# Reordering the engines' queues at two seams of a two-layer decoder trunk, and halving one operand's hand-over

## The reference, cut to what matters

```
h = rms_norm(x, norm_mix_pre);  proj = h @ w_in;   y = [gmlp | retention | swa](proj)
x = x + rms_norm(y @ w_out, norm_mix_post)
h = rms_norm(x, norm_ffn_pre)
x = x + rms_norm((silu(h @ w_gate) * (h @ w_up)) @ w_ffn_out, norm_ffn_post)
x = x + sigmoid(x @ w_ple_gate) * rms_norm(p @ w_ple_proj, ple_norm)
```

## Time and profile before

| | |
|---|---|
| median of 3 runs | 1254.16 us (1253.76 to 1254.63) |
| the profiled execution's own time | 1254.62 us |
| its span in the profile | 1252.1 us |
| busy in the span | PE 1238.4 (99%), PEld 1137.0 (91%), DVE 786.0 (63%), ACT 571.0 (46%), POOL 126.5 (10%) |
| granted TensorE clock | 0.999 of full speed, mean |

### The profile page before, as it was taken

The page is one execution under the profiler, slowest core; times in us unless marked ns, Lnnn a source line. Parts: engine busy times, 40 slices in busy tenths (PEclk is TensorE's granted clock), DMA queues, the critical chain, the costliest instruction groups (busy, mean ns, idle before and its releaser), DMA issues.

```text
span 1252.1 us, 20527 instructions
## 1 busy us (share of the span) xinstructions
PE 1238.4 (99%) x8045; PEld 1137.0 (91%) x8045; DVE 786.0 (63%) x1321; ACT 571.0 (46%) x1084; POOL 126.5 (10%) x225
## 2 busy tenths in 40 slices
PE   9999999999999999999999999999999999999998
PEld 8999887999999988887899989879999999888876
DVE  5675545888888843346466756367988887532463
ACT  6444334555555532235454444353655555322341
POOL 2003521000000000001120037020000000000010
PEclk9999999999999999999999999999999999999999
DMA  7322232233333353423231222222333333523111
GB/s 247 102 66 88 68 101 68 69 102 102 102 109 111 104 167 101 135 68 97 68 98 60 89 64 90 80 81 71 102 103 114 106 102 103 171 89 126 68 51 67
DMA packets 124206, 122.30 MB, mean 98 GB/s; under 512 B 5200, under 2 KB 109008, under 8 KB 124112
## 3 DMA queue, kind: packets, MB, share of 16 engines
q1 hardware_dynamic: 124112, 121.01, 31.4%
HBM read 118.90 MB, written 2.10 MB: 97 GB/s over the span
## 4 chain that ended last, share of the span: by engine, by line
PE 77%; DVE 3%; ACT 2%; issue 1%; POOL 1%; ACTq 0%; DVEq 0%; POOLq 0%
PE bank L799 25%; PE bank L800 24%; PE bank L801 24%; PE bank L989 1%; DVE upd L1838 1%; DVE x L1845 1%; DVE w_lo L1599 1%; PE bank L1046 0%; PE bank L1069 0%; ACT junk L1334 0%; PE bank L1115 0%; POOL tiny L1498 0%; ACT w_hi L1185 0%; ACT junk L1212 0%; PE bank L1067 0%
## 5 line engine op out<-in xcount | busy, mean ns | idle before, releaser
L799 PE MATMUL bank<-w_hi,h_hi 128*128 128x384 f32 (+2 forms) x672 | 244.2, 363 | 1.8 <-DVE ple_n L1838 1.0
L800 PE MATMUL bank<-w_lo,h_hi 128*128 128x384 f32 (+2 forms) x672 | 237.5, 353 | 0.0
L1599 DVE TENSOR_TENSOR w_lo<-raw,w_hi 128x1024 fp32r<-128x1024 f32 x86 | 102.5, 1231 | 157.1 <-ACT w_hi L1185 156.9
L801 PE MATMUL bank<-w_hi,h_lo 128*128 128x384 f32 (+2 forms) x576 | 200.4, 348 | 0.0
L1185 ACT ACTIVATE w_hi<-raw 128x1024 fp32r<-128x1024 f32 x86 | 86.7, 1053 | 181.2 <-PE bank L801 181.1
L799 PE MATMUL bank<-h_hi,w_hi 128*128 128x256 f32 x568 | 161.2, 284 | 3.0 <-issue 1.9
L801 PE MATMUL bank<-h_hi,w_lo 128*128 128x256 f32 x568 | 160.7, 283 | 0.0
L800 PE MATMUL bank<-h_lo,w_hi 128*128 128x256 f32 x568 | 160.7, 283 | 0.0
L799 PEld LDWEIGHTS bank<-w_hi,h_hi 128*128 128x128 f32 x672 | 126.4, 188 | 16.2 <-issue 1.8
L801 PE MATMUL bank<-w_hi,mid_lo 128*128 128x512 f32 x352 | 137.0, 389 | 0.0
L800 PEld LDWEIGHTS bank<-w_lo,h_hi 128*128 128x128 f32 x672 | 126.6, 188 | 10.6
(11 more groups left out here) (235 smaller groups left out, 2662.8 us busy)
## 6 DMA issues: line engine op xcount, KB each, us to landing
raw<-in_w_ffn_in SPq DMA_DIRECT2D x88, 512.0 KB, 3.9
raw<-in_w_ffn_out SPq DMA_DIRECT2D x44, 512.0 KB, 3.4
raw<-in_w_in SPq DMA_DIRECT2D x40, 384.0 KB, 3.8
raw<-in_w_out SPq DMA_DIRECT2D x16, 512.0 KB, 4.0
raw<-in_w_gate SPq DMA_DIRECT2D x16, 512.0 KB, 4.2
raw<-in_w_in SPq DMA_DIRECT2D x10, 512.0 KB, 4.0
raw<-in_w_ple SPq DMA_DIRECT2D x4, 512.0 KB, 4.8
x<-in_x_in SPq DMA_DIRECT2D x3, 512.0 KB, 7.1
```

What stands on the lines that cost most here:

```text
L799: pe.matmul(out_ap, a_hi, b_hi, start=start, stop=False, skip_group_check=True)
L800: pe.matmul(out_ap, a_hi, b_lo, start=False, stop=False, skip_group_check=True)
L801: return pe.matmul(out_ap, a_lo, b_hi, start=False, stop=stop, skip_group_check=True)
L1599: last = dve.tensor_tensor(lo, raw[q % RAWS][:, cols], hi, ALU.subtract)
```

## The change

It moves events in the list, and changes waits:

1. First seam: `conv ffn1` comes before `pre ffn 2` (it was behind it); `post mix 3` comes before `hraw 1`.
2. DVE's `h_lo` of `T ffn 1` is taken out of its own place and put inside `post mix 2`, between the two scaling instructions and the addition to x.
3. The normed tile `xn` is written in two instructions of 512 columns, each with its signal, and PE's transposes wait half by half.
4. `mm_ffn` waits for each of the strip's two pieces and for each half of the tokens' channels (k 0 to 3, k 4 to 7) as it comes to them.
5. Second seam: `conv gate1` moves from behind `T gate 2` to behind `post ple 1`; `conv gate2` from in front of `post ple 2` to behind `post ple 3`.

```diff
@@ tail()
                 if m == TILES - 1 and after == "ffn":
                     add("hraw", 0)
+                    close(pair[0])
             if m >= 1 and after == "ffn":
                 add("pre", after, m - 1, lay=lay)
-            if m == TILES - 1:
+            if m == TILES - 1 and after != "ffn":
                 close(pair[0])
@@ plan_schedule()
         tail(o[2:], ("post", "mix"), "ffn")
+        add("post", "mix", 3)
         add("hraw", 1)
-        add("post", "mix", 3)
...
         mm(ple, 0)
         add("T", "gate", 2)
-        close(fo[-1])
         mm(ple, 1)
         add("T", "gate", 3)
         add("post", "ple", 0)
         mm(ple, 2)
         add("post", "ple", 1)
+        close(fo[-1])
         mm(ple, 3)
-        close(ple)
         add("post", "ple", 2)
         add("post", "ple", 3)
+        close(ple)
@@ mm_ffn()
-                cols = slice(0, S) if m is None else slice(m * S // 2, (m + 1) * S // 2)
+                cols = slice(m * S // 2, (m + 1) * S // 2)
                 for part in range(2):
+                    pe.wait_ge(lo_ready, 2 * g + part + 1)
                     for k in range(KD):
+                        if part == 0 and k % 4 == 0:
+                            pe.wait_ge(h_lo_ready, t_count(layer, "ffn", max(2 * m + 1, j), k // 4))
@@ block_of()
-                if kind != "in":
+                if kind not in ("in", "ffn"):
                     pe.wait_ge(lo_ready, 2 * (g + 1))
...
-                    pe.wait_ge(h_lo_ready, t_count(layer, "ffn", max(2 * m + 1, i)))
@@ transposes()
-                    pe.wait_ge(xn_ready, n)
...
+                    if stage == "ffn":
+                        pe.wait_ge(xn_ready, 2 * n - 1 + half)
@@ pre() on GpSimd
-                    pool.wait_ge(xn_ready, xn_count(layer, m) - 2)
+                    pool.wait_ge(xn_ready, 2 * xn_count(layer, m) - 4)
@@ pre() on VectorE
-                done(dve.scalar_tensor_tensor(out=xn[(xn_count(layer, m) - 1) % 2][:], in0=x[:, m, :],
-                                              scalar=r_pre[n % 2], in1=pre_w[:], op0=ALU.mult, op1=ALU.mult), xn_ready)
+                for c in (slice(0, 512), slice(512, D)):
+                    done(dve.scalar_tensor_tensor(out=xn[(xn_count(layer, m) - 1) % 2][:, c], in0=x[:, m, c],
+                                                  scalar=r_pre[n % 2], in1=pre_w[:, c],
+                                                  op0=ALU.mult, op1=ALU.mult), xn_ready)
@@ VectorE's walk
-                elif kind == "T" and (layer, *e) != (0, "T", "mix", 0):
+                elif kind == "T" and (layer, *e) != (0, "T", "mix", 0) and e[1:] != ("ffn", 1):
...
-                        step(last)
+                        if (stage, m) == ("mix", 2):
+                            written = done(last, dve_step)
+                            split_T(layer, "ffn", 1)
+                            landed(written)
+                        else:
+                            step(last)
                         spent["upd"] = done(dve.tensor_tensor(x[:, m, :], x[:, m, :], upd[:], ALU.add), x_new)
```

## The result

The changed kernel took 1246.71 us (median, 1246.33 to 1246.74) against 1253.96 (1253.69 to 1254.63) on the same chip, a ratio of 0.9941 with a 95% interval of 0.9929 to 0.9953: 7.25 us won of the 8.3 forecast.

A forecast was written before the change was run, and what follows sets the result against it. PE, busy 99%, was taken to bound the kernel, so only its gaps (9.84 us) could be won. Terms 0.63 + 1.20 + 0.80 + 0.74 + 0.76 = 4.13 a layer, 8.3 in all, gave 1245.9 us from 1254.16; range 1244.3 to 1248.5.

The forecast's parts named there:

- The halves, 0.63: First seam, T ffn 0 and 1: xn in halves lets transposes and POOL's root run earlier, 0.63 us a layer.
- POOL nothing: Rival: POOL gains nothing from the seam between halves, 0.30 a layer for 0.63, time 1246.6 us; chance 0.15.
- ffn 0, 1.20: First seam: h_lo of T ffn 1 inside post mix 2 removes the stall before ffn 0, 1.20 us a layer.
- margin of 1.8: T ffn 2: its xn half is there at 222.2, PE wants it at 224.0, despite the later x_new of tile 2.
- ffn 2, 0.80: First seam: the new order and needing only the first w_lo piece remove ffn 2's stall, 0.80 us a layer.
- Margin 0.4, the thinnest of all: Before ffn 2: first w_lo piece done at 231.0, needed by the shifted PE at 231.4.
- margin lost: Rival: no 0.4 margin before ffn 2, or a ple stall moves to gate 0; 0.8 a layer lost, 1247.5 us; chance 0.07.
- The second seam, 1.50: Moving conv gate1 and conv gate2 removes stalls at ple tile 3 (0.74 a layer) and gate 0 tile 2 (0.76).
- Satisfied waits, nothing: 24 more waits in ffn blocks and 8 in transposes cost PE nothing; bound 0.05 each, 1.6 in all.
- The two rivals that price them: Satisfied waits cost PE 0.05 each: 1247.5 us, or 1248.2 if POOL also gains nothing; chance for waits 0.06.
- no change: Rival: no change that shows, needing 6 of the 8 us to fail at both seams; chance 0.04.
- slower: Rival: conv ffn1 on ACT waits for a late raw piece, delaying T ffn 2; 1256.7 us or more; chance 0.03.

The follow-up runs named there:

- Experiment 1: The changed kernel with the normed tile xn written by one instruction again: 1247.65 us, ratio 0.9948.
- experiment 9: The kernel before with only the waits by halves and pieces in the plain ffn blocks added: 1251.73 us, ratio 0.9981.
- experiment 2: The changed kernel with h_lo of T ffn 1 back behind the addition to x: 1246.91 us, ratio 0.9943.
- Experiment 6: The changed kernel with the second w_lo of strip ffn 1 moved behind xn 2 on DVE: 1246.25 us, ratio 0.9936; run again, 1245.86 us.
- 10: The changed kernel with the second w_lo of strip ffn 1 behind xn 2 and h_lo of T ffn 1 back behind the addition to x: 1246.93 us.
- Experiment 5: The kernel before with only conv gate1 moved behind post ple 1, conv gate2 left in place: 1254.58 us, a single execution.
- experiment 7: The kernel before with only the normed tile in halves added: 1253.49 us, ratio 0.9994.
- experiment 8: The changed kernel with conv ffn1 behind pre ffn 2 and hraw 1 ahead of post mix 3 again: 1250.24 us, ratio 0.9971.

## Why the prediction was right, and where not

- **PE's gaps are what can be won: right.** Everything won came from gaps at the seams; the fall of the span, 7.2, is the sum of the gaps that closed.
- **The halves, 0.63: 0.55.** The mechanism held, POOL's part too: its two instructions take 0.47 and 0.84 beside `xn` 0 and 0.39 and 0.84 beside `xn` 1, where 0.4 and 0.8 were forecast. A half takes 0.75 and the pair 1.42, where I took 0.72 and 1.34; so the second half is 0.08 late at each tile. Experiment 1 undoes it for 0.63 a layer. The rival "POOL nothing" (0.30) is out.
- **ffn 0, 1.20: right in size, credited to the wrong part.** Its stall is gone, but the half-wise wait, which the prediction called cover for nothing more, takes about half of it alone (experiment 9), and the move of `h_lo` the other 0.6. `x_new` of tile 2 came later as said, and T ffn 2 kept 1.0 of its margin of 1.8. But the late `x_new` wasn't free: ACT's squares began 0.03 after it, and experiment 2 has them, and with them the `w_lo` of ffn 2, 0.2 sooner. Experiments 6 and 10 repeat it: `w_lo` of ffn 2 begins 23.11 after the seam's start with the move and 22.93 after it without. The prediction priced this delay at T ffn 2 only and not at ffn 2.
- **ffn 2, 0.80: 0.31; this is the step that failed, "Margin 0.4, the thinnest of all".** On PE's side the prediction wrote 231.79 + 0.79 - 1.20 = 231.4 and left out the 0.63 that its own term for the transposes gives PE; PE was ready at 230.91. On DVE's side it let the whole chain begin 1.2 earlier, `w_lo` at 229.8; it began at 230.09, since POOL's root lay under a `w_lo` and `x_new` of tile 2 was late. So the margin of 0.4 was -0.4. The prediction had `conv ffn1` fill the time in which DVE waited for POOL, and didn't ask what the filling does to POOL, though the same rows that gave it the gain of the halves show it. Experiment 6 takes the hold away and 0.32 of the 0.49 with it. For the remaining 0.17, PE is ready at 230.80 there and the first piece at 229.65 + 1.22 = 230.87; the 0.2 of the late `x_new` is more than what is missing. The rival "margin lost" named this, at 0.8 a layer: it happened, at 0.5. The prediction also listed a stall at ffn 2 among the signs that it is wrong, and by that sign its account of this place is wrong, although the time lies within the range.
- **The second seam, 1.50: right.** The working of the second term was too easy: POOL's root before `ple_n` 2 was held there as well, on this row of the changed kernel's timeline:

```profile
581.52 1.76 POOL L1502 TENSOR_SCALAR tiny<-tiny 128x1 f32<-128x1 f32 x1 [2.10 <-ACT junk L1340]
```

  An instruction that takes 0.30 while DVE is idle took 1.76 under two `w_lo` (580.85 to 583.20); `ple_n` 2 began at 584.03, with 0.4 in hand for gate 0 tile 2 (an estimate: its two instructions end at 584.03 + 1.41 = 585.44, PE comes to the tile at about 585.99, and in the kernel before PE started 0.14 after that end) instead of 1.4. Experiment 5 shows the same hold with the margin gone.
- **Satisfied waits, nothing: right.** The stretch above has no hole, and experiment 9 carries the 24 of the ffn blocks with only gains. The 8 in the transposes are not priced by themselves; T ffn 2 and 3 flow without a loss in the changed kernel. The two rivals that price them are out, and "no change" and "slower" with them.
- **The parts don't add up.** Undone one at a time from the changed kernel, order, waits, halves and the move of `h_lo` cost 1.79, 1.09, 0.63 and 0.19 a layer, 3.70 for a seam that won 2.08. One chain on DVE ends at ffn 2 and catches what any part sets free before it: the halves alone give 0.22 (experiment 7), the move of `h_lo` gives 0.19 with the stall at ffn 2 and 0.53 without (experiments 2 and 10). The order is the largest part because it shortens that chain most: `w_lo` of ffn 2 begins 23.43 after the seam's start in the changed kernel, 25.20 after it with the old order (experiment 8) and 24.05 with `xn` whole (experiment 1). Added to the kernel before, the halves shorten it by 0.23 only, from 24.38 to 24.15.

The sum missed 1.1 us of 8.3, and 1246.7 lies inside the range of 1244.3 to 1248.5. The time alone would have spoken for the rival "POOL nothing" (1246.6) rather than for the forecast (1245.9); it is the losses at each place, and experiments 1 and 6, that put the miss at ffn 2.

## What to carry to other kernels

When a gain upstream moves the bound engine earlier, take it off every margin downstream in the same sum; a stall that closes hands its time to the next chain that is just in time. Before filling an engine's idle time with moved work, ask who computes during that idle time and whether the filling slows it: here the filling of DVE's wait lengthened the POOL instruction that it waited for, and a split of the filling in two gave a third of a microsecond back. And judge a part by removing it from the finished version as well as by adding it to the old one: the two gave 0.63 and 0.22 for the same edit.

## What the runs showed of the hardware

- **When POOL gets in between two DVE instructions.** A POOL instruction of 0.2 to 0.3 us started under a DVE instruction with two SBUF inputs ends 0.08 to 0.18 after it (219.95, 1.08 is one), and isn't held by one that reads a bank (0.30 at 580.47 of the kernel before, under `ple_n`, which reads one). At the boundary between two such instructions it depends on the case: between the halves of `xn` it ended 0.17 or 0.18 after the first in all six places of the changed kernel (one is the 0.47 of the POOL rows above), and it ended just behind the first of two `w_lo` when started 0.17 after that one's start (the mixers) and when started 1.04 after it (219.76, 0.25 in experiment 2; there the next POOL instruction, 0.57 alone, took 1.40). But the one started 0.67 after the start of the first of two `w_lo` was held by both (581.52, 1.76), in both layers and in every run with the second seam's moves, and so was that of experiment 5 (1.54, and 1.52 in layer 1), which began 0.90 after the start of the third of four. What decides was not found. The prediction's "POOL gets in at the seam of two DVE instructions" holds for the halves and not in general. In the GPSIMD Engine Reference, section 1 (Specifications), the Trainium skill has GpSimd share its SBUF interfaces with VectorE, contended by DVE instructions with two SBUF inputs. The traces agree that it is such DVE work that holds POOL, with 1.76 for 0.30 as the worst seen here.
- **Halving costs 0.14 a tile.** `xn` takes 1.28 whole, and 1.42 as a pair of 0.75 each that overlap by 0.08. The formula that the prediction took from VectorE: DVE Perf Modes of the Trainium skill, section "The TRN2 errata", gave 0.69 for a half, an estimate. The traces agree for a sum of two SBUF operands of 512 columns (0.69, `T_sum` at 233.24 in the kernel before) and show 0.06 more for this scale-and-multiply.
- **The profiler's brackets** understate as told in the prediction: at ffn 2 the bracket says 0.25 where the starts say 0.49.
